# Attention stage of a hybrid decoder: sample exponential behind two evacuations, and two weight tiles moved from the value products to the prompt steps

## What is computed

```python
z, xbc, dt_raw, q, k, v, g_ssd, g_attn = split_cols(u @ w_in, IN_SIZES)
xbc_full = jnp.concatenate([conv_state, xbc], axis=1)
conv = conv_b + sum(xbc_full[:, i:i + seqlen] * conv_w[i] for i in range(CONV_WIDTH))
conv = jax.nn.silu(conv)
...
logits = jnp.einsum('bthe,btjhe->bthj', q, kg) * ATTN_SCALE + bias      # samples: cache and new keys
lse = jax.nn.logsumexp(logits, axis=-1)
p = jnp.exp(logits - lse[..., None])
o = jnp.einsum('bthj,btjhe->bthe', p, vg)
...
logits = jnp.einsum('znqhe,znkhe->znhqk', qb, kb) * ATTN_SCALE + bias   # prompt, by blocks of 128
p = jnp.exp(logits - lse[..., None])
o = jnp.einsum('znhqk,znkhe->znqhe', p, vb)
```

## Time and profile before

| | |
|---|---|
| median of 3 runs | 2303.55 us (2298.8 to 2303.8) |
| the profiled execution's own time | 2308.41 us |
| its span in the profile | 2306.7 us |
| PE, DVE, ACT, POOL busy | 88%, 58%, 39%, 18% |
| mean granted TensorE clock | 0.944 of full |

### The profile page before, as it was taken

One profiled execution on the slowest core, in us unless ns is written; L12 is line 12 of the kernel. 1 busy time (PEld: TensorE's weight loads), 2 busy tenths in 40 slices (PEclk: granted clock), 3 DMA queues, 4 the chain that ended last, 5 costly groups with the idle time before them and its releaser, 6 DMA issues.

```text
span 2306.7 us, 38377 instructions
## 1 busy us (share of the span) xinstructions
PE 2039.0 (88%) x14960; PEld 1901.6 (82%) x14960; DVE 1347.9 (58%) x2087; ACT 889.0 (39%) x1071; POOL 425.6 (18%) x214
## 2 busy tenths in 40 slices
PE   6999899886888888999999999989688888979996
PEld 4999898875676788999989998878577667979996
DVE  3663546774777482665366544578577774446643
ACT  3332434443444532433343233444443345233322
POOL 3000002211333455100000000121123334630000
PEclk9999999987999999999999999998899999989998
DMA  7544455422344333444444445444334443434541
GB/s 198 174 164 152 131 185 171 153 74 81 118 133 126 110 109 127 159 163 147 148 163 164 154 147 173 154 144 131 90 91 121 123 121 104 146 123 158 166 157 57
DMA packets 258912, 317.64 MB, mean 138 GB/s; under 512 B 9375, under 2 KB 233487, under 8 KB 258676
## 3 DMA queue, kind: packets, MB, share of 16 engines
q1 hardware_dynamic: 249912, 288.07, 38.8%
q0 software_dynamic: 8192, 27.05, 4.1%
q10 hardware_dynamic: 680, 0.80, 0.1%
HBM read 291.91 MB, written 26.65 MB: 138 GB/s over the span
## 4 chain that ended last, share of the span: by engine, by line
PE 70%; DVE 13%; ACT 5%; issue 4%; POOL 3%; DVEq 2%; DMA 2%; ACTq 0%; SPq 0%; POOLq 0%
PE ps L1568 20%; PE ps L1570 19%; PE ps L1569 19%; PE ps L1700 4%; POOL w_lo L1459 3%; ACT w_hi L711 3%; DVE w_lo L983 2%; DVE flat L1405 1%; PE ps L1970 1%; DMA w_raw<-in_ffn_w_dram 1%; PE ps L1657 1%; DVE acc L1211 1%; DVE acc L1214 1%; DVEq L1217 1%; PE ps L1990 1%
## 5 line engine op out<-in xcount | busy, mean ns | idle before, releaser
L1568 PE MATMUL ps<-u_hi,w_hi 128*128 128x288 f32 x2736 | 840.0, 307 | 54.5 <-DVE u_lo L1010 16.0
L1569 PE MATMUL ps<-u_lo,w_hi 128*128 128x288 f32 x2736 | 823.2, 301 | 0.0
L1570 PE MATMUL ps<-u_hi,w_lo 128*128 128x288 f32 x2736 | 819.8, 300 | 0.0
L711 ACT ACTIVATE w_hi<-w_raw 128x2048 fp32r<-128x2048 f32 x249 | 476.4, 1913 | 786.3 <-PE ps L1570 772.1
L983 DVE TENSOR_TENSOR w_lo<-w_raw,w_hi 128x2048 fp32r<-128x2048 f32 x174 | 398.4, 2290 | 331.5 <-ACT w_hi L711 331.2
L1568 PEld LDWEIGHTS ps<-u_hi,w_hi 128*128 128x128 f32 x2736 | 529.4, 193 | 68.3 <-issue 18.6
L1569 PEld LDWEIGHTS ps<-u_lo,w_hi 128*128 128x128 f32 x2736 | 530.1, 194 | 0.7
L1570 PEld LDWEIGHTS ps<-u_hi,w_lo 128*128 128x128 f32 x2736 | 530.5, 194 | 0.0
L1459 POOL TENSOR_TENSOR w_lo<-w_raw,w_hi 128x2048 fp32r<-128x2048 f32 x75 | 348.2, 4643 | 535.6 <-ACT w_hi L711 534.9
L1568 PE MATMUL ps<-h_hi,w_hi 128*128 (+1 forms) x704 | 209.2, 297 | 15.5 <-DVE w_lo L983 15.5
L1570 PE MATMUL ps<-h_hi,w_lo 128*128 (+1 forms) x704 | 207.9, 295 | 0.0
(11 more groups left out here) (308 smaller groups left out, 2544.0 us busy)
## 6 DMA issues: line engine op xcount, KB each, us to landing
w_raw<-in_ffn_w_dram SPq DMA_DIRECT2D x128, 1024.0 KB, 5.0
w_raw<-in_w_in_dram SPq DMA_DIRECT2D x82, 1024.0 KB, 5.2
h<-in_state_ssm_dram SPq DMA_DIRECT2D x32, 512.0 KB, 4.1
out_dram<-h POOLq DMA_DIRECT2D x32, 512.0 KB, 4.0
w_raw<-in_w_ssd_out_dram SPq DMA_DIRECT2D x16, 1024.0 KB, 4.8
kv_in<-in_cache_kv_w_dram SPq DMA_DIRECT2D x32, 256.0 KB, 4.6
w_raw<-in_w_o_dram SPq DMA_DIRECT2D x8, 1024.0 KB, 4.9
w_raw<-in_ffn_w_dram SPq DMA_DIRECT2D x8, 512.0 KB, 3.5
```

Of the source, the lines that this page charges most:

```text
L711: act.activation(w_hi[s][:], raw[s][:], ACT.Copy).then_inc(hi_ready[s].sem, 1)
L1568: pe.matmul(out, wh, hi, start=first, stop=False)
L1569: pe.matmul(out, wh, lo, start=False, stop=False)
L1570: return pe.matmul(out, wl, hi, start=False, stop=last)
```

## The change

In the softmax ScalarE copies out tiles 12 and 13, with the high half and the silu that follow tile 13, before it waits for the maximum and takes the exponential. `XBC_VALUES` goes from (3, 2, 3, 2) to four times 2, so two tiles leave the value products. The prompt has eight tiles, 24 to 31, in place of six: tile 24 stands between the first scores and the turn of the sample output, and tiles 25 to 31 stand in steps 1 to 7. Before, tiles 26 to 31 stood in steps 1 to 6. VectorE's count `left` is 4 before and after.

```diff
--- before.py
+++ after.py
@@ -99,8 +99,8 @@
 XBC_START = 2
 XBC_KEYS = (2, 3, 2, 3)
 XBC_SOFTMAX = (3, 1)
-XBC_VALUES = (3, 2, 3, 2)
-XBC_PROMPT = (0, 1, 1, 1, 1, 1, 1, 0)
+XBC_VALUES = (2, 2, 2, 2)
+XBC_PROMPT = (1, 1, 1, 1, 1, 1, 1, 1)
 XBC_UNITS = 2 * PAIRS_XBC
 assert XBC_START + sum(XBC_KEYS + XBC_SOFTMAX + XBC_VALUES + XBC_PROMPT) == KC
 SIDE_TILES = 3 * G
@@ -839,10 +839,11 @@
                     key_tiles(2 * n + 1)
                     for _ in range(XBC_KEYS[n]):
                         q = xbc(q)
-                wait(act, max_s_ready, l, 1)
-                act.activation(sc_s[:], sc_s[:], ACT.Exp, bias=stat_s[0][:], accum_out=stat_s[1][:])\
-                    .then_inc(exp_s_ready.sem, 1)
-                for _ in range(XBC_SOFTMAX[0]):
+                for n in range(XBC_SOFTMAX[0]):
+                    if n == 2:
+                        wait(act, max_s_ready, l, 1)
+                        act.activation(sc_s[:], sc_s[:], ACT.Exp, bias=stat_s[0][:], accum_out=stat_s[1][:])\
+                            .then_inc(exp_s_ready.sem, 1)
                     q = xbc(q)
                 wait(act, pt_s_turned, l, 1)
                 act.activation(st[:, 0:3, :], ps[:, 4, 0:3 * P].rearrange("p (k c) -> p k c", k=3), ACT.Copy)
@@ -863,6 +864,7 @@
                         .then_inc(exp_p_ready.sem, 1)
 
                 exponentials(0)
+                q = xbc(q)
                 for n in range(2 * HPG):
                     k = n % 2 + 1
                     wait(act, pt_p_turned, l, n + 1)
@@ -871,7 +873,7 @@
                                    ACT.Copy).then_inc(pt_p_ready.sem, 1)
                     if n + 1 < 2 * HPG:
                         exponentials(n + 1)
-                    for _ in range(XBC_PROMPT[n]):
+                    if n:
                         q = xbc(q)
                 xbc_silu(XBC_UNITS - 1)
                 act.drain()
@@ -1234,7 +1236,7 @@
                 dve.drain()
                 dve.tensor_scalar(sc_s[:], sc_s[:], stat_s[2][:], None, ALU.mult).then_inc(p_s_ready.sem, 1)
                 done = (XBC_START + sum(XBC_KEYS)) // 2
-                left = sum(XBC_PROMPT) // 2 + 1
+                left = sum(XBC_PROMPT) // 2
                 for n in range(done, XBC_UNITS - left):
                     xbc(n)
                 wait(dve, v_done, l, 1)
@@ -1899,8 +1901,8 @@
                         for kt in range(k):
                             last = turn(ps[:, 4 + kt, g * P:(g + 1) * P], sc_p[n % 2][:, g, kt * P:(kt + 1) * P])
                     last.then_inc(pt_p_turned.sem, 1)
-                    for t in range(XBC_PROMPT[n]):
-                        xbc(q + sum(XBC_PROMPT[:n]) + t)
+                    if n:
+                        xbc(q + n)
                     wait(pe, pt_p_ready, l, n + 1)
                     half = slice(64 * (i % 2), 64 * (i % 2) + 64)
                     for g in range(NG):
@@ -1911,6 +1913,7 @@
                     last.then_inc(o_p_ready.sem, 1)
 
                 scores(0)
+                xbc(q)
                 sample_out()
                 for n in range(2 * HPG):
                     if n + 1 < 2 * HPG:
```

## The result

The changed kernel takes 2341.7 us (median of 6 runs, 2339.64 to 2344.99) where the kernel before takes 2300.64 in runs beside it: a ratio of 1.0182, 95% interval 1.0165 to 1.020. It is slower, by 41.1 us. The forecast was 2341, 37.4 above the median of 2303.55 that stood for the kernel before. The profiled execution took 2344.07, with a span of 2342.4 (before 2306.7: 35.7 more) and a mean granted clock of 0.937 (before 0.944).

What follows compares the result with a forecast made beforehand. One chain through three engines was taken to set the pace, with TensorE idling in it. Per layer 6.4 + 5.6 + 4.7 + 1.5 + 1.5 + 2.1 - 3.1 = +18.7, for two +37.4: 2341 us, range 2326 to 2355.

Steps and rivals of the forecast that it cites:

- The softmax: Sample weights' turn at 417.2 in place of 422.02, TensorE idle 3.8 us, next tile 1.5 slower: 3.2 us sooner.
- that rival: Softmax table load on ScalarE at the page's price: exponential 1.4 us later per layer, 2344 in all; chance 0.03.
- The start of step 1: Prompt step 1 begins 3.1 us sooner per layer, bounds 0 to 5.9.
- the third value product: End of value stage: tile 23 behind three value products, not two (1.21 each), shrinking the 3.2 us gain to 2.0.
- this wait: VectorE's 1.10 us wait at the late turn of the sample output, ahead of step 1, would go.
- The odd steps: Steps 1, 3, 5 to the next turn: tile, copy, high half, convolution without overlap; +6.4, +5.6, +4.7 us per layer.
- the two prices of a turn and tile: Turn plus tile on TensorE in an odd step: 6.21 us at half clock, 4.01 at full clock.
- The cold clock: After idling 6 us or more, TensorE runs steps 2 and 6 cold, +1.5 us each; step 4 paid already.
- The rival of a clock that stays low: Clock low through all prompt steps: 2.2 us more in steps 3, 5 and 7, 2354 in all; chance 0.10.
- Behind the last step: From step 7's turn to the last silu: tile 31, high half, GpSimd's low half of unit 17; 14.9 us, +2.1.
- Faster: Rival: tiles vanish in TensorE's idle time in the prompt steps, at most 5.9 us gained per layer, 2292; chance 0.05.
- no change: Rival: prompt-step losses no more than the 3.1 us gained, VectorE late in odd steps by another cause; chance 0.04.

Runs made afterwards that it cites:

- e8: The changed kernel run once more, with nothing altered: 2343.43 us, ratio 1.0182 to the kernel before.
- e11: The changed kernel with all odd low halves of the attention stage made by VectorE in place of GpSimd: 2321.99 us, ratio 1.009 to the kernel before.

## Why the prediction was right

**The softmax.** Forecast: turn at 417.2 behind 3.8 us of idling. It came at 416.63 behind 3.69, which is 417.05 on the clock of before. The exponential starts 1.29 after its table load's start (413.67 to 414.96). By an estimate with the drain that the Trainium skill's page "ScalarE: Activation LUTs", section "What ACT_TABLE_LOAD costs", adds, it would have been 416.3: the row was right here, and that rival falls.

**The start of step 1.** This is the term that was mis-sized: forecast 3.1 us sooner, measured 478.37 - 473.09 = 5.3. VectorE reached the scores of step 0 at 465.45, 3.1 sooner, where I had 2.0. Of that, 0.4 is the earlier start of the stage. Counted from the convolution of unit 5 (410.11 before), VectorE comes there after 58.40 us before, 55.00 with the softmax alone, 59.17 with the tiles alone and 55.76 in the changed kernel: the softmax gave 3.4 where I had 3.2, and the moved tiles took 0.8 where I had 1.2 for the third value product.

The other 2.2 are TensorE's. Before, the late turn of the sample output (`st`) stood between VectorE's start on step 0 (468.51) and TensorE's scores of step 1, and these ran at half clock:

```profile
469.94 1.12 PE L1700 MATMUL ps<-square,st 128*128 128x128 f32 x4 [2.69 <-ACT st L855]
470.99 2.93 PE L1891 MATMUL ps<-qkv 64*128 64x256 f32 x6
```

Now the scores start 0.67 behind VectorE (466.12 - 465.45) in place of 2.48 (470.99 - 468.51): 1.8 sooner, where I had 1.1 for this wait. They took 1.56 at full clock, which I had not priced, but only 0.4 of that counts, since the turn of step 0 then waits for VectorE:

```profile
468.59 0.87 PE L1702 MATMUL ps<-square,sc_p 128*128 128x128 f32 x3 [0.91 <-DVE sc_p L1281]
```

In the first layer of e8, the second profile of the changed kernel, the same scores took 2.93 again, and still the turn of step 0 came 3.53 behind VectorE's start, against 3.14 here and 5.33 before. So the wait that went is the larger part, and the clock the smaller.

**The odd steps.** Forecast +6.4, +5.6, +4.7; measured +6.5, +5.3, +4.7 in the first layer. The pieces can be checked one by one in step 1: turn to the end of the tile 479.28 - 473.09 = 6.19 (forecast 6.21), from there to the end of the high half 481.65 - 479.28 = 2.37 (2.37), and low half to turn 488.70 - 481.69 = 7.01 (7.00). In step 3 GpSimd took 4.50 where the row of before had 4.60. In the second layer step 1 took 13.43, since tile 25 ran at full clock there: 1619.93 - 1615.93 = 4.00 from turn to output, 2.2 us less, the difference between the two prices of a turn and tile that the range had used.

**The cold clock.** Forecast +1.5, 0, +1.5 behind the even turns; measured +1.3, +0.6, +2.0 in the first layer and +2.6, -0.2, +1.5 in the second: 3.9 and 3.8 in all, where 3.0 were forecast. The waits ahead of the three steps are the same in both layers, so their length does not tell how this falls on the steps. The rival of a clock that stays low falls: step 3 took 499.32 - 495.33 = 3.99 from turn to output, and the forecast had 4.01.

**Behind the last step.** Forecast +2.1, measured +3.0: the turn stands at 538.03 and the silu at 553.84, 15.81 apart, where 14.9 were forecast. GpSimd did stop VectorE, but at an earlier instruction than I thought, the split of the attention output (544.50, 5.11 us), so that the rest of it, the copy of tails and the whole convolution came behind the stop: from GpSimd's end (544.49 + 4.50) to the silu 4.85 us, where 3.85 were forecast.

**The sum.** In the first layer -5.3 + 6.5 + 1.3 + 5.3 + 0.6 + 4.7 + 2.0 + 3.0 = 18.1, which is 553.84 - 535.74; forecast was 18.7. The gain that was too small and the losses that were too small by 0.9 (clock) and 0.9 (end) nearly cancel: the mechanism was right, and the closeness of the total is in part luck. In the second layer the stage grew by 16.3. The 2341 is close to 2341.7 by luck once more: 37.4 were forecast and 41.1 measured between medians, but the kernel before took 2300.64 beside it, 2.9 less than the median that the forecast started from. The two profiled executions differ by 35.7.

**Faster, or no change.** Both asked for the high half of unit 14 to stand ready when VectorE comes to it. VectorE waited 6.80 us for it. In the kernel with the tiles ahead of the steps it does stand ready, and that kernel is not slower than before.

## What to carry to other kernels

Moving work into another engine's idle time is safe only where its consumer comes later in every engine's order. Write down, for each engine that works in order, which step consumes the moved tile, and if that is the step in which it now stands, add up the chain (tile, copy, next operand, consumer) as one line without overlap. An engine that is busy 45 of 46 us need not be the bound: look at who reads its last result, and when. And a helper engine's work can cost its neighbour more than the work itself.

## What was unexpected of the hardware

The split of the attention output took 5.11 us in the changed kernel, against 0.76 before and 0.76 in e11. Before:

```profile
530.92 0.76 DVE L995 TENSOR_TENSOR attn_lo<-attn,attn_hi 128x576 fp32r<-128x576 f32 x1
```

In the changed kernel GpSimd's low half began 0.01 us ahead of it (544.49) and ended at 548.99; VectorE's row ends at 549.61, 0.62 later, about its own length. It reads two inputs from SBUF. The two instructions share no tile, and neither waits for a semaphore of the other, so the engines here do not wait for each other through semaphores alone. The Trainium skill's page "SBUF — State Buffer", section "Who interferes with whom", says that a VectorE instruction with two SBUF inputs contends with a GpSimd instruction that reads SBUF, and that the order of issue decides who is stopped: the trace agrees. In e11, where GpSimd makes no low half, the row is back at 0.76.

GpSimd's help was a loss in this stage on the whole. A low half takes it 4.5 to 4.9 us there, and VectorE, when a copy of tails, the first instruction of a convolution or this split falls into it, stands still for the rest of it; VectorE itself needs 2.29. Not every instruction is stopped: in the low half from 493.64 of the kernel before, a maximum (0.55) and a copy out of PSUM (0.29) ran at their usual length. And where VectorE had nothing to do, behind the last step of the kernel before, the help was free. Giving it all eight made the kernel before faster (0.9973) and took half of the loss off the changed one (1.009 for 1.0182).

The clock's recovery differs where the code is the same: from its turn to the next, step 1 took 15.61 us in the first layer and 13.43 in the second of the same execution, and 15.42 and 14.83 in the second profile (e8). What decides it was not tried.
